# One decoder kernel, four edits: index columns first, remainders in float32r, three weight units before the index keys, features released by halves

## Time and profile before

| what | us |
| --- | --- |
| median of 3 runs | 1618.36 |
| lowest and highest | 1614.49, 1620.58 |
| the profiled execution, its own time | 1620.47 |
| its span, first to last instruction | 1618.7 |
| mean granted TensorE clock | 0.984 of full |

### The profile page before, as it was taken

How to read it: one execution, slowest core, us unless ns; L and a number is a source line. 1 busy time by engine, 2 the same in 40 slices (tenths; PEclk the granted TensorE clock), 3 DMA queues, 4 the chain that set the end, 5 groups by cost and what they waited for, 6 DMA issues and landing times.

```text
span 1618.7 us, 30649 instructions
## 1 busy us (share of the span) xinstructions
PE 1556.1 (96%) x11772; PEld 1415.8 (87%) x11772; DVE 883.4 (55%) x1534; ACT 683.5 (42%) x995; POOL 276.4 (17%) x474
## 2 busy tenths in 40 slices
PE   6999989999999999999999998899999999999998
PEld 5787746999999999999977776479999999999998
DVE  6668884245555553222857688624455555432345
ACT  4444556244444442224443444644444444322241
POOL 3420340111111110100115105202111111101000
PEclk8999999999999999999999999999999999999999
DMA  5233144123333233322222511332233323333221
GB/s 166 66 99 87 34 142 110 53 66 91 91 90 89 80 87 100 92 81 85 79 69 77 138 40 58 105 98 86 72 91 91 91 78 91 98 88 92 84 70 61
DMA packets 225719, 140.24 MB, mean 87 GB/s; under 512 B 13122, under 2 KB 219604, under 8 KB 225552
## 3 DMA queue, kind: packets, MB, share of 16 engines
q1 hardware_dynamic: 223220, 133.46, 28.3%
q0 software_dynamic: 2400, 5.42, 1.0%
HBM read 131.21 MB, written 7.65 MB: 86 GB/s over the span
## 4 chain that ended last, share of the span: by engine, by line
PE 79%; DVE 13%; ACT 3%; issue 3%; POOL 1%; DMA 0%; DVEq 0%; SPq 0%; ACTq 0%; POOLq 0%
PE ps L1714 23%; PE ps L1716 22%; PE ps L1715 22%; DVE score L1379 3%; DVE m L1376 3%; DVE w_L L1270 2%; PE ps L2065 1%; PE ps L1994 1%; DVE Lb L1451 1%; PE ps L1741 1%; PE ps L1797 1%; PE ps L1905 1%; PE ps L1767 1%; PE ps L2149 1%; PE ps L1907 1%
## 5 line engine op out<-in xcount | busy, mean ns | idle before, releaser
L1714 PE MATMUL ps<-bH,w_H 128*128 128x272 f32 x1664 | 481.1, 289 | 4.7 <-DVE w_L L1270 3.2
L1270 DVE TENSOR_TENSOR w_L<-w_raw,w_H 128x1024 fp32r<-128x1024 f32 (+4 forms) x236 | 257.6, 1100 | 414.1 <-ACT w_H L890 411.3
L1716 PE MATMUL ps<-bH,w_L 128*128 128x272 f32 x1664 | 479.6, 288 | 0.0
L1715 PE MATMUL ps<-bL,w_H 128*128 128x272 f32 x1664 | 477.9, 287 | 0.0
L890 ACT ACTIVATE w_H<-w_raw 128x1024 fp32r<-128x1024 f32 (+4 forms) x236 | 220.1, 943 | 270.1 <-PE ps L1716 269.4
L1714 PEld LDWEIGHTS ps<-bH,w_H 128*128 128x128 f32 x1664 | 312.6, 188 | 6.3 <-DVE w_L L1270 4.1
L1715 PEld LDWEIGHTS ps<-bL,w_H 128*128 128x128 f32 x1664 | 313.6, 188 | 0.1
L1716 PEld LDWEIGHTS ps<-bH,w_L 128*128 128x128 f32 x1664 | 312.6, 188 | 0.0
L1714 PE MATMUL ps<-actH,w_H 128*128 128x272 f32 x704 | 204.2, 290 | 0.0
L1716 PE MATMUL ps<-actH,w_L 128*128 128x272 f32 x704 | 203.8, 289 | 0.0
L1715 PE MATMUL ps<-actL,w_H 128*128 128x272 f32 x704 | 202.7, 288 | 0.0
(11 more groups left out here) (343 smaller groups left out, 2326.6 us busy)
## 6 DMA issues: line engine op xcount, KB each, us to landing
w_raw<-in_w_up SPq DMA_DIRECT2D x88, 512.0 KB, 3.7
w_raw<-in_w_down SPq DMA_DIRECT2D x32, 512.0 KB, 3.9
w_raw<-in_w_in SPq DMA_DIRECT2D x24, 512.0 KB, 5.0
w_raw<-in_w_ple_gate SPq DMA_DIRECT2D x16, 512.0 KB, 3.9
w_raw<-in_w_down SPq DMA_DIRECT2D x16, 384.0 KB, 3.4
w_raw<-in_w_out SPq DMA_DIRECT2D x16, 320.0 KB, 3.5
w_raw<-in_w_in SPq DMA_DIRECT2D x8, 452.0 KB, 4.0
w_raw<-in_w_in SPq DMA_DIRECT2D x8, 384.0 KB, 3.6
```

The lines of the kernel that those rows point to most:

```text
L1270: ins = dve.tensor_tensor(w_L[u % SPLIT][:, a:b], w_raw[raw_slot(l, u)][:, a:b], w_H[u % SPLIT][:, a:b].bitcast(F32), ALU.subtract)
L1714: pe.matmul(out, wh, xh, start=start, stop=False)
L1715: pe.matmul(out, wh, xl, start=False, stop=False)
L1716: return pe.matmul(out, wl, xh, start=False, stop=stop)
```

## The change

- **Index first.** The chunks are reordered: the 452 columns with the indexer come first, the 512 of A's queries and keys second. The index rows are rotated and transposed during the second chunk, and the index products, relu and weighing stand in it too, no longer between the features. The squares of the heads are made by ScalarE from the accumulator, as a second instruction of `leave`; VectorE only sums. GpSimd multiplies the gains into the rotation tables once per layer (six instructions) and then has one multiplication per token tile where it had three. `rotate` for `qk` uses the two tables, one group of heads after the other, six multiplications per tile where there were three.
- **Rounds.** 13 stand before the pair loop, 21 in it, 6 after it, and 8 in the softmax steps, two in each of the first four.
- **Remainders.** `Lb` is split like a weight: ScalarE rounds it (`stick_high`), VectorE subtracts (`stick_low`), and `remainders` goes over both parts in float32r. Before the first remainders of pairs 0 and 1 TensorE now has one more half of a feature unit.
- **Units 16 to 18** are loaded before the pages of index keys.
- **Halves.** `feature_out` takes each half in an instruction of its own, and the next unit's first half can begin when the first half is out.
- Both decode steps stand together, and the second waits for the raw unit's load and no longer for its split.

```diff
-CHUNK = [(0, 512), (512, 964), (1732, 2116)]
+CHUNK = [(512, 964), (0, 512), (1732, 2116)]
-        I_BANK = [7, 0]
+        I_BANK = [3, 4]
 (SyncE)
+                for u in range(16, 19):
+                    load_unit(u)
                 sp.wait_ge(rope_ok, at(rope_ok, 10))
...
-                for u in range(16, U_OUT + RAW):
+                for u in range(19, U_OUT + RAW):
 (GpSimd, per token tile)
-                    pool.tensor_tensor(x, x, hstat..., ALU.mult)
-                    pool.tensor_tensor(x[:, 0:6, :], x[:, 0:6, :], gains...)
-                    pool.tensor_tensor(x[:, 6:8, :], x[:, 6:8, :], gains...).then_inc(qk_ok, 1)
+                    pool.tensor_tensor(x, x, hstat..., ALU.mult).then_inc(qk_ok, 1)
 (ScalarE)
+                        copy(x_tok[0:n, t, :], src, r)
+                        ins = act.activation((t1, t2)[t % 2][0:n, :], src, ACT.Square, scale=r)
...
+                def stick_high(h):
+                    act.wait_ge(b_dve, at(b_dve, 4 * (h // 2) + h % 2 + 1))
+                    if h >= 2:
+                        act.wait_ge(b_o, at(b_o, h - 1))
+                    copy(L_high[:, h % 2, :], Lb[:, h % 2, :]).then_inc(b_act, 1)
 (VectorE, head_squares)
-                    dve.scalar_tensor_tensor(t1[0:n, :], x_tok[0:n, t, :], 1.0 / HD, x_tok[0:n, t, :], ALU.mult, ALU.mult)
                     dve.tensor_reduce(hstat[0:n, t, :], ...)
 (VectorE, projection to features; the new order)
+                split(7)
+                weigh(1, 0, 2)
+                weigh(1, 2, 4)
+                select(1, 0, 2)
+                split(8)
+                weigh(2, 0, 2)
+                weigh(2, 2, 4)
+                select(1, 2, 3)
+                weigh(3, 0, 2)
+                weigh(3, 2, 4)
+                select(1, 3, 4)
+                head_squares(0)
+                split(9)
...
+                split(10)
+                select(1, 4, 7)
+                split(11)
+                qk(0)
+                qk(1)
+                split(12)
...
+                select(1, 7, 9)
                 feature_out(1)
                 split(15)
+                select(1, 9, 13)
 (VectorE, pair loop)
+                def stick_low(h):
+                    dve.wait_ge(b_act, at(b_act, 4 * (h // 2) + h % 2 + 3))
+                    lo(L_low[:, h % 2, :], Lb[:, h % 2, :], L_high[:, h % 2, :]).then_inc(b_dve, 1)
...
+                stick_low(4)
+                stick_low(5)
                 split(21)
...
-                select(3, 7, 13)
+                select(3, 2, 8)
 (VectorE, softmax steps)
-                    if u < 3:
-                        select(3, 13 + u, 14 + u)
+                    if u < 4:
+                        select(3, 8 + 2 * u, 10 + 2 * u)
 (TensorE)
+                    for part in (L_high, L_low):
+                        for i in range(4):
+                            mm = pe.matmul(bz(h, i), ntri_r, b_blk(part, h, i), ...)
+                    for part in (L_high, L_low):
+                        for i in range(3):
+                            for j in range(i + 1, 4):
+                                mm = pe.matmul(bz(h, i, P * (j - i)), nones_r, b_blk(part, h, j), ...)
...
+                            if c == 1 and t == 1:
+                                if k in (2, 4):
+                                    turn(0, 1 if k == 2 else 4)
+                                elif k > 4:
+                                    index(k - 4, 2)
...
+                        if c == 1 and k in (4, 5, 6):
+                            index(k - 3, 0)
```

More of the change, by code:

```diff
@@ L990, in _ @@
                 part_copy(0)
-                for t in range(TILES):
+                leave(0, 0)
+                split(5)
+                for t in range(1, TILES):
                     leave(0, t)
-                split(5)
-                act.wait_ge(hs_ss, at(hs_ss, 1))
-                inverse(hstat[:, :, :], hstat[:, :, :]).then_inc(hs_rec, 1)
                 act.wait_ge(u_tr, at(u_tr, 1))
@@ L1027, in _ @@
                     leave(2, t)
-                for t in range(1, 4):
-                    relu(t, 0, 4)
-                    split(U_F + t + 1)
+                turned(1, 0)
+                turned(1, 1)
+                split(14)
+                turned(1, 2)
+                turned(1, 3)
+                split(15)
+                turned(1, 4)
+                split(16)
                 def stick_exp(h):
@@ L1066, in _ @@
                     stick_ln(e1, r1)
-                    split(U_F + 2 * q + 5)
                     if q == 0:
@@ L1405, in _ @@
                 dve.wait_ge(hs_one, at(hs_one, 1))
+                index(0)
+                split(5)
+                index(1)
+                index(2)
+                split(6)
+                index(3)
+                index(4)
+                split(7)
[7 more added lines that the diff above has]
+                weigh(3, 0, 2)
@@ L1866, in feature @@
                         mm = tri_product(ps[:, F_BANK[n] + half, 0:HALF], H[:, wk], Lo[:, wk], aH[:, k, x], aL[:, k, x], k == 0, k == KD - 1)
[L1867 to L1870 removed]
+                    if k1 == KD:
+                        mm.then_inc(w_used if half else f_mm, 1)
+                for n in range(3):
                     for half in range(2):
[L1872 to L1879 removed]
+                        feature(n, half)
+                        if 2 * n + half < 4:
+                            turn(1, 2 * n + half + 1)
                 def logits(q):
[L1884 removed]
+                    pe.wait_ge(f_ev, at(f_ev, 4 * q + 4 if q else 6))
                     if q == 0:
@@ L1933, in _ @@
                     feature(2 * q + 3, 1)
+                    if q < 2:
+                        feature(2 * q + 4, 0)
                     remainders(2 * q)
```

266 lines of the change are left out of this document (131 added, 135 removed).

## The result

The changed kernel takes 1625.4 us (median of 9 runs, 1622.8 to 1629.2); the kernel before 1618.4 in as many. The ratio of after to before is 1.0048, 95% interval 1.0029 to 1.0068. So it is slower by 7 us or 0.5%, where I had forecast 2.4 us less. The profiled execution has a span of 1623.6 us against 1618.7, 4.9 more; 3.1 of them are there when the FFN of the first layer begins.

What follows compares the result with a forecast made beforehand. VectorE and TensorE were taken to fill the pair stage, VectorE alone the first softmax steps. Per layer -3 - 5.3 + 8.7 = +0.4, against 1.5 less contention, taken as -1, -2 in all: 1616 us, range 1601 to 1628.

Steps and rivals of the forecast that it cites:

- -3 ahead of the pair stage: Before the pair stage: TensorE's stall and low clock go, VectorE ends earlier; -3 us per layer, bounds -5 and +3.
- +2 for VectorE's waits in the pair stage: Pair stage: VectorE waits 2 us more per layer on the longer latency from logits to remainders.
- -1.5 for less contention: GpSimd's shorter work no longer slows normalisations and rotations; about 1.5 us saved per layer.
- Softmax steps, +8.7 per layer: First softmax steps: five added rounds of 1.74 us count in full, VectorE being the bound; lower +2, upper +11.
- rival 2: Softmax steps hide the rounds, costing 3 us instead of 8.7; 1605 us, down to 1592; chance 0.27.
- Pair stage, -5.3: Pair stage: fewer rounds outweigh VectorE's new subtractions, copies, halves and waits; -5.3 us per layer, bounds -12 and 0.
- expected TensorE wait of 4 us in pair 2: Pair stage: no half feature covers the remainders' latency in pair 2, so TensorE stands for 4 us.
- signs that I had named: Pair stage, among others: TensorE less busy by 10 us or more, stage 5 shorter, no VectorE wait beyond 2 us.
- 60 columns less, then 60 more, no gain: Projection chunks 0 and 1 only swap their widths, which was to gain nothing.
- rival 1: GpSimd's pooling means hold up VectorE's subtractions, about 5 us per layer; 1626 us, up to 1632; chance 0.19 with its ring.
- no slack: Pair stage: the 12.7 us in which VectorE is not busy are hops between instructions, not free time.
- Halves and early units, 0: Features taken by halves and early units 16 to 18 come to nothing, at most 1 us of waits hidden each.

Runs made afterwards that it cites:

- e4: The changed kernel with the five extra rounds per layer in the softmax steps left out, so three remain there; 1608.7 us.
- e1: The changed kernel with five of its eight softmax rounds per layer put back ahead of the softmax stage; 1618.1 us.
- e14: The changed kernel with the split of weight unit 12 ahead of the second query-key rotation on VectorE instead of behind it; 1620.8 us.
- e15: The kernel before with two parts of the change alone, early loads of units 16 to 18 and features by halves; 1620.1 us, ratio 1.0016.
- e9: The changed kernel with float32 remainders again and all 16 rounds over 512 scores ahead of the softmax stage; 1607.2 us, ratio 0.9929 to before.
- e11: The changed kernel with four filler products instead of two after each of the first five softmax steps; 1626.4 us.
- e10: e9 with the split of weight unit 12 moved ahead of the second query-key rotation on VectorE; 1604.0 us, ratio 0.9916 to before.
- e12: e1 with the remainders of the last pair, heads 4 and 5, in float32 again; 1613.2 us.
- e6: e1 with the remainder subtractions of heads 0 to 3 moved from VectorE to GpSimd; 1622.8 us.

## Why the prediction was wrong

That VectorE bounds the pair stage and the first softmax steps was right. Three terms of the sum failed: -3 ahead of the pair stage, which TensorE's waits for low weights ate up in layer 0; +2 for VectorE's waits in the pair stage, which were 3.8; and -1.5 for less contention, of which nothing reached the time. I had -2 us for the profiled execution and it was +4.9; the medians moved by +7.

**Softmax steps, +8.7 per layer: right.** First row maximum to decode products: 37.9 to 47.0 in layer 0 (+9.2), 37.5 to 45.1 in layer 1 (+7.6). e4 prices the five rounds at 8.4 each layer, and rival 2, the only one that made the kernel faster, falls with it: in the steps that hold the rounds VectorE waits for another engine once, 0.56 us at 210.57 ahead of the first round, and it did so before.

**Pair stage, -5.3: measured -3.0 in both layers.** The failing term is the one for waits. I took 2 us for the longer latency from logits to remainders; VectorE's waits rose from 1.5 to 5.3 us, so 3.8. The rest of the term's sum, 7.3 us less of work and hops, came as 6.9. None of the five waits stands at a subtraction. Two are at a first clamp behind ScalarE's logarithm (2.15 us at 187.73, 0.85 at 163.56), one behind TensorE at feature 4 (1.14), one at a split behind ScalarE (0.71), one is VectorE's own (0.50). The rounds that were moved out had filled this time: with five of them back the waits are 2.1 (e1). The expected TensorE wait of 4 us in pair 2 came as 3.9, with a cold clock behind it. A head took 2.8 us instead of 2.4, which can't be seen to matter in a stage where TensorE stands for 7.7. Of the signs that I had named, TensorE was to be less busy by 10 us (7.1) and no wait of VectorE over 2 us (2.15).

**Ahead of the pair stage, -3: measured 0.0 in layer 0 and -2.7 in layer 1.** The stall of 2.9 us at 69.8 went, as foreseen, and the 1.7 us of low clock behind it. What I missed stands at 109.69: chunk 2 is now followed by features whose low weights wait behind two rotations on VectorE, the first of which was slowed by GpSimd. That wait of 1.5 us is in both layers, and the ring of the index products adds one of 0.9 (0.3 before). A third is in layer 0 alone:

```profile
35.05 0.71 PE L1767 MATMUL ps<-w_H,aH 128*128 128x452 f32 x1 [2.51 <-DVE w_L L1302]
```

VectorE makes the low parts of the activations there up to 33.8 us and only then splits unit 2. Before, TensorE came to that unit at 35.7, from products 512 columns wide and with the first decode step (1 us) ahead of it; now it comes at 32.5, because the first chunk has 60 columns less and the decode steps stand further back. "60 columns less, then 60 more, no gain" was therefore a loss in layer 0: the columns saved are waited out, those added are paid. Without it the terms are -2.9 - 1.7 + 1.5 + 0.6 = -2.5, near the -2.7 of layer 1; with it they are 0.0, as in layer 0. All 14 profiled executions with the new order have this wait, of 1.3 to 2.7 us, and none of the 3 with the old one. No run puts a decode step back to test it.

Single executions pin these figures only to a microsecond or two. From the first product of the projection to the first logits twelve executions of the new order took 109.2 to 110.8 us in layer 0 and 106.8 to 108.4 in layer 1; three of the old one took 110.4 to 110.9 and 108.7 to 112.9. My layout of the new order ran on VectorE alone and never asked for each split when TensorE would need it. By e14 the split behind two rotations is worth 3 to 6 us of the 7.

**Less contention, -1.5 per layer: nothing of it in the time.** The lengthening itself did shrink. Before, VectorE's instructions between 62 and 78 us took about 8 us more than the same forms without GpSimd at work; after, those between 99.57 and 104.5 took 3.2 more (the split at 99.57 2.56 against 1.03, two products of the first rotation 1.39 and 1.19 against 0.56 and 0.35). But the part of it ahead of the stall at 69.8 is already in the term for that stall, and behind it VectorE waited for ScalarE anyway (2.9 us at 85.8, 2.4 at 95.4, 3.5 at 107.6), while the new lengthening stands just ahead of the split that TensorE waits for at 109.69. Whatever it brought is inside the measured stages, so nothing is left for a term of its own.

The rule that I cited from the Trainium skill ("SBUF — State Buffer", section "Who interferes with whom") fits what the trace shows at the split of 99.57, at that of 194.13 and at the subtractions too, where it works against GpSimd. These began first and kept their length (2.91 us for two), and GpSimd's instructions that began beside them took 1.39 and 2.28 us where the same forms a few microseconds earlier took 0.21 and 1.26:

```profile
187.31 0.21 POOL L805 TENSOR_TENSOR first<-pw,con 64x16 f32<-64x16 f32 x1
187.71 1.26 POOL L809 TENSOR_TENSOR pooled<-pooled,u_p 64x496 f32<-64x496 f32 x1 [0.18 <-POOL first L805]
...
191.47 1.39 POOL L805 TENSOR_TENSOR first<-pw,con 64x16 f32<-64x16 f32 x1
193.04 2.28 POOL L809 TENSOR_TENSOR pooled<-pooled,u_p 64x496 f32<-64x496 f32 x1 [0.18 <-POOL first L805]
```

The split at 194.13 began while the last of these was still at work and was the one held up. So rival 1 had the rule right and the order of the starts wrong. Starts less than a tenth of a microsecond apart don't tell the order: before, GpSimd's 64x32 multiplication at 198.23 grew from 0.36 to 1.46 us and the split at 198.26 kept its 1.22.

**A round was misread, without harm.** I called all beyond the 0.43 us of MAX8 the hop. The kernel before, one round over 512 scores:

```profile
189.48 0.68 DVE L1376 MAX8 m<-score 128x8 f32<-128x512 f32 x1
190.31 0.09 DVE L1379 MATCH_VALUE_LOAD score<-m,score 128x8 f32 x1
190.39 0.68 DVE L1379 MATCH_REPLACE8 score<-m,score 128x512 f32<-128x512 f32 x1
191.21 0.69 DVE L1376 MAX8 m<-score 128x8 f32<-128x512 f32 x1
```

Of 1.73 us from start to start 1.45 are instructions and 0.28 are hops, and as much at the other widths. Over 39 rounds that is 11 of the 12.7 us in which VectorE was not busy, so "no slack" stands.

**Halves and early units, 0: perhaps a cost** (e15, interval up to 0.33%; its pair stage is 1.6 us longer in layer 0 and 0.2 in layer 1).

**Not of the change, -3.1 in layer 0.** Between the decode and the FFN the profiled execution of before spent some microseconds at the low clock, that of after none. First this stretch of before, then the same of after, with the same work in both:

```profile
250.50:347.70 97.20, 96.28 (x945) 83.18 (x945) 36.42 (x72) 41.63 (x71) 10.21 (x10) 0.96 0.32 90
```

```profile
256.70:350.80 94.10, 93.03 (x944) 80.07 (x945) 36.40 (x72) 41.63 (x71) 10.24 (x10) 1.00 0.35 93
```

In the 17 profiled executions the stretch of layer 0 from the first index-score product of the decode to the square sum of the FFN took 94.1, 95.7 or 97.3 us (each within 0.1), at a clock of 1.00 (after), 0.98 (e1, e9, e11) or 0.96 (before, e10, e12), in three groups that don't follow the kernel; before fell into the longest and after into the shortest. This may be why the spans differ by 4.9 us where the medians differ by 7; it is not shown.

With these, over both layers, -2 becomes +3.3 (ahead) + 4.6 (pair stage) - 0.6 (softmax) + 3 (contention) - 3.1 (clock) = 7.2 more, +5.2, beside 4.9 measured.

**The chances.** Rival 1 (1626) came within 1 us of the measured time, and that is luck: its held subtractions don't exist, and the means cost 2.3 to 3 us per layer, not 5, and as much in the kernel before. The forecast's flaw was to count every part's saving at its own engine and to ask too little what a fixed order makes the other engine wait.

## What to carry to other kernels

Where two engines fill a stage together, an edit that trades one's work for the other's has no price of its own: the single passes were worth -6, 0, +11 or, on the kernel before and with the halves and the order that go with them, +23 us, by how much else stood on VectorE. Ask which engine waits for which in the stage (the brackets of the timeline, for both), and move what can move, here the rounds, to the engine's waits and away from the stage where it alone is the bound; that, without the new arithmetic, gave 1604 us. And for each instruction that is moved in a fixed order, check who is waiting for the one behind it.

## What the runs showed of the hardware

Four float32r passes over 1280 columns take 0.65 us from start to start and six over as many 0.75, so a narrow pass costs more than its share of columns. A subtraction of 128x1280 float32 takes 1.45 us on VectorE and 2.94 on GpSimd (e6). Where instructions of the two engines with both inputs in SBUF meet, the one that began clearly first kept its length and the other grew: the split at 194.13 from 1.22 to 2.27 us, GpSimd's instructions at 191.47 and 193.04 by 1.2 and 1.0 beside the subtractions, and its second subtraction in e6 by 1.0 beside the split of 145.66. VectorE's normalisations, with one such input, grew beside the means too, from about 0.5 to 1.49 and 1.10 us. With the rounds in the softmax steps a granted clock of 0.80 in place of 0.59 gave back nothing (e11).
